# The recurrent stage's token-major operands laid out by direction, its products joined in pairs, and the gating rows requested ahead of the feed-forward loops

## What is computed

```
g, u = split(x @ w_in);  ffn = (silu(g) * u) @ w_out                 # twice in the first block
m_x = silu(c) @ mod_w + mod_b ;  m_c = silu(c_ctx) @ mod_w + mod_b   # 48 slabs of mod_w
# recurrence, 8 heads of 64, per direction d, 256 context then 512 latent positions:
s = s * w_t - (s kk_t) (kk_t a_t)^T + v_t k_t^T ;  y_t = s r_t       # y only for the latent positions
y = y_forward + y_backward
```

## Time and profile before

| | |
|---|---|
| three runs | 3107.16 us in the median, 3104.86 to 3117.13 |
| profiled execution | 3118.53 us, of which the span is 3116.9 us |
| TensorE, VectorE, ScalarE, GpSimd busy | 90%, 57%, 45%, 27% of the span |
| mean granted clock of TensorE | 0.95 |
| feed-forward output loops | begin at 259 and 1506 us |
| recurrence, chunk by chunk | 2143 to 2457 us |

### The profile page before, as it was taken

The page is one execution under the profiler, slowest core; times in us unless marked ns, Lnnn a source line. Parts: engine busy times, 40 slices in busy tenths (PEclk is TensorE's granted clock), DMA queues, the critical chain, the costliest instruction groups (busy, mean ns, idle before and its releaser), DMA issues. The chain is left out here.

```text
span 3116.9 us, 53002 instructions
## 1 busy us (share of the span) xinstructions
PE 2816.6 (90%) x20916; PEld 2297.6 (74%) x20916; DVE 1773.3 (57%) x2734; ACT 1417.7 (45%) x1913; POOL 850.6 (27%) x515
## 2 busy tenths in 40 slices
PE   9999999998989899999997999997877688799996
PEld 7887877776768687788774787776777465688884
DVE  3115456788999642311445402446776554699996
ACT  4445545555663232444344222334433222588884
POOL 3444451220004343344432234222332131000001
PEclk9999999999999999999998999997998788899997
DMA  3225371112222132222552122221000023899996
GB/s 125 94 95 188 135 280 64 42 61 66 80 81 98 61 122 88 88 94 95 187 189 85 54 75 85 75 78 52 5 4 4 29 81 115 326 412 411 412 411 243
DMA packets 110379, 412.30 MB, mean 132 GB/s; under 512 B 12064, under 2 KB 12080, under 8 KB 109312
## 3 DMA queue, kind: packets, MB, share of 16 engines
q1 hardware_dynamic: 88560, 322.24, 28.4%
q0 software_dynamic: 11136, 48.26, 4.2%
q10 hardware_dynamic: 10512, 39.33, 3.5%
HBM read 370.45 MB, written 39.32 MB: 131 GB/s over the span
## 5 line engine op out<-in xcount | busy, mean ns | idle before, releaser
L219 POOL TENSOR_TENSOR ring_r<-ring,whi 128x1024 fp32r<-128x1024 f32 x241 | 591.3, 2463 | 1017.4 <-ACT whi L214 1008.0
L231 PE MATMUL psum<-xn_r,whi 128*128 128x512 f32 x1176 | 460.1, 391 | 0.0
L214 ACT ACTIVATE whi<-ring 128x1024 fp32r<-128x1024 f32 x247 | 256.0, 1054 | 421.1 <-DMA ring<-stream 420.8
L229 PE MATMUL psum<-xh,ring_r 128*128 128x512 f32 x936 | 388.6, 415 | 28.1 <-DVE ring_r L219 20.5
L2813 DVE TENSOR_TENSOR er_r<-er,eh 128x1024 fp32r<-128x1024 f32 x268 | 309.5, 1219 | 1.0 <-ACT eh L2802 0.4
L2802 ACT ACTIVATE eh<-er 128x1024 fp32r<-128x1024 f32 x268 | 268.2, 1072 | 40.3 <-DMA er<-experts 39.6
L2031 PE MATMUL psum<-mem 64*64 64x64 f32 (+1 forms) x7744 | 214.8, 231 | 69.8 <-issue 24.8
L229 PE MATMUL psum<-ffn_xh,ring_r 128*128 128x512 f32 x672 | 261.4, 389 | 0.0
L230 PE MATMUL psum<-ffn_xh,whi 128*128 128x512 f32 x672 | 261.4, 389 | 0.0
L2031 PEld LDWEIGHTS psum<-mem 64*64 64x64 f32 x7744 | 200.8, 145 | 81.2 <-issue 55.1
L231 PEld LDWEIGHTS psum<-xn_r,whi 128*128 128x128 f32 x1176 | 222.1, 189 | 47.3
(11 more groups left out here) (527 smaller groups left out, 6031.3 us busy)
## 6 DMA issues: line engine op xcount, KB each, us to landing
ring<-stream SPq DMA_DIRECT2D x311, 512.0 KB, 3.3
er<-experts SPq DMA_DIRECT2D x276, 512.0 KB, 8.2
mem<-mod_w ACTq DMA_DIRECT2D x48, 512.0 KB, 3.5
xs_dram<-zero_row POOLq DMA_DIRECT2D x1, 12288.0 KB, 41.6
xs<-xs_dram SPq DMA_DIRECT2D x23, 512.0 KB, 8.1
ys_dram<-y_t ACTq DMA_DIRECT2D x23, 512.0 KB, 6.7
spill<-resid POOLq DMA_DIRECT2D x2, 2048.0 KB, 26.6
resid<-spill POOLq DMA_DIRECT2D x2, 2048.0 KB, 9.9
```

The costliest lines, as they stand in the source:

```text
L214: act.activation(high_of(part, j), w, ACT.Copy).then_inc(w_hi, 1)
L219: pool.tensor_tensor(ring_r[:, s, :, :], ring[:, s, :, :], f(high_of(part, j)), ALU.subtract).then_inc(w_lo, 1)
L229: pe.matmul(bank, lo[:, b, :], x_hi_, start=start, stop=False, skip_group_check=True)
L231: return pe.matmul(bank, hi[:, b, :], x_lo_, start=False, stop=stop, skip_group_check=True)
```

## The change

**Feed-forward.** The request of the `c` rows moves from `mod_act` to `ffn_act`, ahead of the input loop. Output slabs 2 and 3 are split right after the four `mod_w` requests, ahead of the wait for the rows; slab 4 + g then follows `mod_w` slab g.

```diff
 def mod_act(act, n):
-    act.dma_start(mod_c, c_rows).then_inc(x_in, 16)
     for m in range(first, first + 4):
         mod_load(act, m, n)
+    for j in (2, 3):
+        split_hi(act, f"ffn{n + 1}_out", j)
     act.wait_ge(x_in, 16 * (n + 1))
...
-        if g < FT - 2:
-            split_hi(act, f"ffn{n + 1}_out", 2 + g)
+        if g < FT - 4:
+            split_hi(act, f"ffn{n + 1}_out", 4 + g)
...
 def ffn_act(act, n):
     x_hi_act(act, 2 * n, ffn_xh)
+    act.dma_start(mod_c, c_rows).then_inc(x_in, 16)
     with act.Fori(0, FT // 2) as i:
```

**Recurrence.** Token-major operands (tokens on the partitions) now hold the forward direction on partitions 0 to 63 and the backward one, its time reversed as it is read, on 64 to 127; the free dimension holds head parity h and pair q. Masks are one 64-column set for both directions. A tile is `(q, h, d)`; channel-major operands sit on row half h, token-major ones on half d:

```diff
+crossed = [(q, h, h ^ w) for q in range(4) for w in (1, 0) for h in range(2)]
+level = [(q, h, d) for h in range(2) for q in range(4) for d in range(2)]
...
+def joint(c, lhs):
+    def tile(q, h, d):
+        w = 2 if emits(c) else 1
+        out = psum[ROWS[d], 4 + h, :].rearrange("p (w q t) -> p w q t", w=2, q=4)[:, 0:w, q, :]
+        moving = KR[c % 3].rearrange("p (w n t) -> p w n t", w=2, n=8)[ROWS[h], 0:w, 2 * q + d, :]
+        return one(out, feat(lhs, q, d)[ROWS[h]], moving)
...
+def turned(bank, v):
+    for q in range(4):
+        ins = pe.transpose(psum[:, bank, q * P:(q + 1) * P], v[:, q * P:(q + 1) * P], ident[:, :])
...
 def lora_pe(c):
-    for m in range(2):
-        for q in range(4):
-            for d in range(2):
-                ins = pe.matmul(psum[:, 2 + d, ...], wlo[m][r, q * P:(q + 1) * P], src)
+    for m in range(2):
+        for q in range(4):
+            ins = one(psum[:, 2 + m, q * P:(q + 1) * P], wlo[m][:, q * P:(q + 1) * P], lwd[:, m, :])
...
-level_Ys(c, 1, state_G_old(s), pe_s)
-alone(state_G_new(s), ALL, pe_s)
+level_Ys(c, 1, state_G_new(s), level, pe_s)
+alone(state_G_old(s), crossed, pe_s)
...
 # VectorE, after state_decay(s)
+if more and emits(n):
+    masked(n, "AT", R2, 1, M_R)
 cumulate(c + 2, 1)
 level_y(c, 5)
 key_mix(c + 2, 1)
-masked(n, "R1", R1, M_R)
 level_x(c, 5)
-masked(n, "R2", R2, M_R)
+masked(n, "CT", CT, 0, M_CT)
+masked(n, "CT", R1, 1, M_R)
```

More of the change, by code:

```diff
@@ L2008, in rwkv_act @@
                     pair_copy(c + 1, "kT", kT)
+                if more:
+                    pair_copy(c + 1, "bT", bT)
                 if c:
@@ L2202, in rwkv_pe @@
                     lora_pe(c + 2)
[L2203 to L2205 removed]
+                for g, part in enumerate((LOW, HIGH)):
+                    alone(level_W(c, 1, g), level[part], pe_l)
                 level_Ys(c, 2)
                 if last:
[L2208 to L2219 removed]
@@ L2220, in rwkv_pe @@
-                w = level_W(c, 3, 0)
-                if last:
-                    z = state_Z(s)
-                    beside(w, LOW, pe_l, z, LOW)
-                    w = level_W(c, 3, 1)
-                    beside(w, LOW, pe_l, z, HIGH, pe_s)
-                else:
-                    alone(w, LOW, pe_l)
-                    alone(level_W(c, 3, 1), LOW, pe_l)
-                if more:
-                    level_Ys(c, 4, pair_kT(n), pe_m)
-                else:
-                    level_Ys(c, 4)
+                    alone(state_U(s), level, pe_s)
@@ new lines, in rwkv_pe @@
+                a = pair_AT(n) if more else None
+                for g, part in enumerate((LOW, HIGH)):
+                    w = level_W(c, 2, g)
+                    if more:
+                        beside(w, level[part], pe_l, a, crossed[part], pe_m if g else None)
+                    else:
+                        alone(w, level[part], pe_l)
+                level_Ys(c, 3)
+                z = state_Z(s) if last else None
+                for g, part in enumerate((LOW, HIGH)):
+                    w = level_W(c, 3, g)
+                    if last:
+                        beside(w, level[part], pe_l, z, crossed[part], pe_s if g else None)
+                    else:
+                        alone(w, level[part], pe_l)
@@ L2257, in rwkv_pe @@
-            s = NCH - 1
-            alone(state_G_old(s), ALL, pe_s)
-            alone(state_G_new(s), ALL, pe_s)
-            alone(state_U(s), ALL, pe_s)
-            alone(state_y_old(s), ALL, pe_s)
-            alone(state_y_new(s), ALL, pe_s)
+                    beside(w, level[LOW], pe_l, state_y_old(s), crossed, pe_s)
+                    alone(state_y_new(s), crossed, pe_s)
+                else:
+                    alone(w, level[LOW], pe_l)
+                alone(level_W(c, 4, 1), level[HIGH], pe_l)
@@ new lines, in rwkv_pe @@
+                level_Ys(c, 5)
+                k = pair_CT(n) if more else None
+                for g, part in enumerate((LOW, HIGH)):
+                    w = level_W(c, 5, g)
+                    if more:
+                        beside(w, level[part], pe_l, k, crossed[part], pe_m if g else None)
+                    else:
+                        alone(w, level[part], pe_l)
+                if more:
+                    turned_v(n)
+            s = NCH - 1
+            alone(state_G_new(s), level, pe_s)
@@ L2263, in rwkv_pe @@
+            alone(state_G_old(s), crossed, pe_s)
+            alone(state_U(s), level, pe_s)
+            alone(state_y_old(s), crossed, pe_s)
+            alone(state_y_new(s), crossed, pe_s)
             rwkv_out_pe(pe)
```

390 lines of the change are left out of this document (185 added, 205 removed).

## The result

The changed kernel is **slower**: 3144.5 us in the median of four runs (3139.1 to 3156.9) against 3106.9 of the kernel before on the same chip (3104.9 to 3117.1), ratio 1.0108 with a 95% interval of 1.0086 to 1.0131. The forecast was 3081, 26 us faster; it is 38 us slower by the medians, 34 by the ratio. The profiled execution took 3156.9 us with a span of 3155.3, 12.4 above the median; that of the kernel before was 11.6 above its own, so differences between the two traces can be read against those of the medians.

| stretch of the span, us | before | after | difference |
|---|---|---|---|
| start to chunk 0 | 2153.0 | 2136.5 | -16.5 |
| twelve chunks | 295.2 | 348.5 | +53.3 |
| rest | 668.7 | 670.3 | +1.6 |

The account below looks back on a forecast made before the run. TensorE was taken as the bound, losing time in output-loop waits and in recurrence stops read as instruction fetch. Terms -9.4 -5.3 -11 = -25.7 us took 3107.2 to 3081, range 3058 to 3102.

Parts of the forecast that it names:

- First loop: First feed-forward output loop: TensorE's 7.04 us wait and the half-speed stretch behind it go, -9.4 us.
- Second loop: Second feed-forward output loop: its 6.0 us wait and some 2.3 us of slow clock go, less 3 at the end, -5.3 us.
- The 3 us given back at its end: Second output loop's end: two more slabs follow the last split, costing 2.4 to 3.7 us, taken as 3.
- Stops are instructions: Recurrence: stops without a semaphore read as TensorE out of instructions; "issue" idle to fall from 25 us to under 8.
- the third rival: Recurrence: stops aren't instruction fetch and stay, +29 us, 3110 us in all; chance 7%.
- Prices of the lists: Recurrence: charges for matmul lists, such as 1.84 us for level tiles beside joined products and -0.93 us for y_new.
- The rival that quarters don't overlap: Recurrence: a matmul bound for a busy quarter holds all behind it; 3.7 us per joined list, loop +31, 3123 us; chance 6%.
- my 25.5: Emitting recurrence chunk: forecast at 25.5 us against the mean of 26.6, -1.1 each, -5.5 us for five.
- Clock 1.00 throughout: Recurrence, chunk 8 of the kernel before, 26.1 us: clock at its higher level throughout, the basis for pricing an emitting chunk.
- the mask put in front of level 5's: VectorE's chain after level 4's last W: one more mask ahead of level 5's first, 0.6 us between starts.
- a new wait of over 3 us: TensorE at level 5's W in the recurrence: a new wait over 3 us would show the forecast wrong.
- a rival (3123): Recurrence: the quarters of the array don't overlap as charged, loop +31 us, 3123 us in all; chance 6%.

Follow-up runs that it names:

- e3: The changed kernel plus 8 unused full-array matmuls of 128 columns in TensorE's wait for level 5's mask; 3106.3 us, ratio 0.9996 to the kernel before.
- e6: The changed kernel with that wait filled by 32 matmuls of 64 columns on the two diagonal quarters; ratio 0.9982 to the kernel before.
- e15: The changed kernel with that wait filled by 64 matmuls of 64 columns going round all four quarters; ratio 1.0015 to the kernel before.
- e16: The kernel before with fewer records: from chunk 2 on, products turning v and k cut from 16 matmuls each to one; ratio 0.9991 to the kernel before.
- e4: The changed kernel with VectorE doing level 5's mask before R2's mask, the state's decay and the cumulated sum; 3106.7 us, ratio 0.9996 to the kernel before.
- e7: The kernel before with three more unused VectorE products ahead of level 5's mask in chunks 0 to 10; ratio 1.0108 to the kernel before.
- e5: As e3, the changed kernel with the wait filled, but with 3 full-array matmuls instead of 8; ratio 1.0009 to the kernel before.
- e11: The changed kernel with G_old (four quarters) back beside level 1 and G_new (two quarters) alone behind it; ratio 1.0079 to the kernel before.
- e9: The kernel before with only the feed-forward parts changed, plus 24 full-array matmuls in chunk 0 and 6 ahead of level 1 in chunks 10 and 11; 3095.7 us, ratio 0.9955.
- e13: As e6, the changed kernel with the wait filled, but with 64 one-column matmuls on the two diagonal quarters; ratio 1.0265 to the kernel before.

## Why the prediction was wrong, point by point

- **Output loops: the waits went as forecast, and the second loop gave more.** First loop: TensorE's products behind the old wait stand 8.8 us earlier than before, and ahead of it they stood 0.7 us later, so 9.5; forecast 9.4. Second loop: the lead is 9.9 us ahead of it and 17.7 at the first product behind the residual (1616.67 against 1634.39), so 7.8 against 5.3 forecast, outside the 4.6 to 5.9 given. The 3 us given back at its end were too many: the wait for the residual is 7.51 us, not 10. The lead is 19.5 us by 1657, where the kernel before ran some products at the lower clock, and 16.5 at chunk 0.
- **Stops are instructions: right.** From 2182 to 2497 us, from within chunk 1 to 12 us behind the loop, the instruction queue moves 53 packets for 6778 records, 128 a packet (the rows below). On the stretch that the earlier trace rows has for before, chunk 2 to 9 us behind the last one (here 2197.9 to 2494), it is 50 packets for 6366 records, where 52 or 53 were forecast instead of 63:

```profile
q8 instruction: 53, 0.87, 1.1%
...
2182.00:2497.00 315.00, 274.69 (x6778) 256.83 (x6773) 173.84 (x492) 92.88 (x203) 75.62 (x106) 0.77 0.01 3
```

  Stops went from 14.5 to 2.9 us in chunks 5 to 9, and over the twelve chunks from 28.6 to 6.1 (forecast: under 8). So the third rival, by which the stops stay, is refuted, and e3, e6, e15 and e16 show that they go with the number of instructions. That the stops are the fetch itself, and not another cost of the same instructions, is the reading that fits, not shown apart. The Trainium skill, "Runtime: NRT & Kernel Launch", section Instruction fetch mechanics, calls the fetch hidden; if the stops are the fetch, it was not hidden here, with 14.5 us of stops in 133.2 us.
- **Prices of the lists: right at full clock.** In e3 W of level 5 beside the joined CT takes 2.03 us for 64 records (forecast 1.84 of issue and 0.2 for the last one's length), W of level 2 beside AT 1.87 with its gaps, y_new 1.00 instead of 1.82. The rival that quarters don't overlap is wrong: it had 3.7 us for such a list. Around transposes in e3, from the last start of one kind of tile to the first of the other, 0.15 to 0.20 us pass, no more than charged. The Trainium skill, "TensorEngine Tiling (Array Packing)", section Key Properties, says that a change of tiling mode drains TensorE; whether these 0.15 to 0.20 us are that drain no run here shows apart, and at this price it decides nothing. An emitting chunk at full clock is 24.5 us in e3, 23.7 in e4, below my 25.5. Two slips changed little: (2.05 - 0.27)/15 is 0.119 us a record, not 0.115, and in the rival that quarters don't overlap the context chunks were priced at 1.3 us in the sum and at 2 in the sentence before it.
- **The clock: the step that failed.** "Clock 1.00 throughout" was read off chunk 8 of the kernel before and carried into a stream with a fifth fewer records; the sum has no term for a clock that falls more. I had priced the mask put in front of level 5's (0.6 us) as a delay alone, and named a new wait of over 3 us there as a sign of being wrong. The wait came to 2.07 us, below that sign, and yet behind it TensorE stood at half clock for 13.7 us in six chunks and for 10 to 17 in most others. So the loop came out 53 us longer where 11 us less had been forecast. The slow stretch is worth about 5.6 us of a chunk (30.7 less the 25.1 of e3), 49 us in the loop (340.8 less 292.2) of the two profiled executions; the medians of the change and e3 differ by 38 us. About 7 us of the loss lie in chunk 0 (29.0 against 21.7), which e3 and e4 don't repair.
- **The forecast's range** left this out. No rival had the clock as its mechanism, though the rows of before showed it at 0.93 in the recurrence and at 0.50 behind a 7 us wait. The time came nearest to a rival (3123) whose mechanism the runs refute.
- **Not settled:** what decides whether the clock falls behind a wait and when it returns. Longer waits in a denser stream did less harm (e7), shorter ones in the thin stream hardly any in chunks 5 to 9 (e4: 3.4 us at the lower clock against 64.5), and chunks with the same program differ (e5, e11).

## What to carry to other kernels

Where TensorE runs small tiles with waits between them, work taken off it is not a saving until the granted clock of the new stream is known: price every wait once as a delay and once with the half clock that may follow. When a change makes TensorE's stream thinner, look at which wait its slack collects in, move that operand to the front of the other engine's order, and if it can't be moved, fill the wait with matmuls whose result nobody uses; in the old layout, whose clock stayed up more, such filling brought nothing (e9). Stops without a semaphore in lists of small matmuls call for fewer instructions, and show only after that what the next limit is.

## What the runs showed of the hardware

- Adding 88 full-array matmuls (1.85 us a chunk) to the changed kernel made it 35 us faster (e3).
- Filling the wait with matmuls of 64 columns on two quarters of the array left 35.3 us of the loop at the lower clock (e6), with full-array ones 48.9 (e3), with one-column ones 219.5 (e13). In e13 the clock fell at 2423.46, 1.2 us into the second row below, while TensorE ran them; as they also ran past the wait, what they do to the clock is not separated from the delay.
- A one-column fp32 matmul on a 64x64 tile, weight load included, costs as much as one of 64 columns: 29 ns a record at full clock on two quarters. The first of these rows is e13's first 14 records, then come a stop and the rest, about two thirds of them at the lower clock:

```profile
2421.29 0.60 PE L2055 MATMUL psum<-shared 64*64 64x1 f32 x14
2422.25 5.06 PE L2055 MATMUL psum<-shared 64*64 64x1 f32 x111 [0.35 <-issue]
```
